# RWKV features and scan in one block: decays inverted tile by tile, scan products waiting for one operand

## Chip, cores and metric

The kernel runs on one core of one Trainium2 chip. The metric is the device time of one execution in microseconds (us). A profile of one execution stands beside it. Engines are named as in the profile: PE (TensorE matmul), PEld (its weight loads), DVE (VectorE), ACT (ScalarE), POOL (GpSimd), SP (SyncE).

## The reference, cut to what matters here

The kernel computes one layer of a hybrid diffusion backbone. The change lies in its RWKV-7 branch, which is run first over 256 context tokens and then over 512 latent tokens, in both time directions. Per token, the features are a decay, a rate `a`, a normalised key `kk` and an effective key:

```
w_log = -softplus(-(w0 + tanh(wd) @ w_up)) - 0.5
decay = exp(-exp(w_log));  a = sigmoid(a0 + ad @ a_up)
kk    = k * k_k, normalised per head of 64
k_eff = k * (1 + (a - 1) * k_a)
step: S = S * decay - (S @ kk) kk*a + v k_eff ;  out = S @ r
```

The context scan yields only a state, which is where the latent scan starts.

## The kernel before, in words

There are 4 `PAIRS` of heads (128 partitions each) and 2 directions, `g` or `z` = 0 and 1. Time is cut into chunks of C = 64 tokens: 4 for the context (names ending in `_c`), 8 for the latent tokens (`_x`).

`phase_rwkv_features` (line 533) works through 8 units n = (z, c), direction 0 first. For each unit PE projects (L596, L598), ACT takes two tanh (L569, L571) and an exponential that is the decay `w` (L577), and DVE runs `decay(n)`, a running product of the decays into `b.G` (L638), and `rates(n)`, which turns `qa` into `(1 + tanh) * kk` (L649). The line for the effective key, `ke`, is made on POOL for direction 0 (L615) and on ACT for direction 1 (L582). Units 4 to 7 are direction 1; DVE does `decay`, `rates` for each in turn. G has 65 columns per chunk, because each product starts with a 1.

`phase_rwkv_scan` (line 675) is a block of its own. Before its first chunk, POOL's `prepare(0, g)` makes for each direction, each product waiting for the one before it: `p` (kk times G, into `pr`), in the latent scan also `rho`, then `kf` (ke times k), and, once DVE has inverted the chunk's G into `ginv` (L991, `reciprocal` over all 4 pairs, 128x256), `q` (qa times ginv, into `qs`) and `k` (kf times ginv, into `ks`), both at L782. Direction 0's products all stand ahead of direction 1's in POOL's queue, and DVE's inversion of direction 1 waits for the `start` that POOL gives behind direction 0's products.

PE then multiplies, in the order Q of g 0, Q of g 1, K of g 0, K of g 1 (L915): Q has `qs` and K has `ks` as stationary operand, both `pr` as moving one. Its waits all stand ahead of the Q product of a direction, and the one on POOL is for that direction's `k`, POOL's last product. Behind them come DVE masks (L1003 to L1012), transposes (L889), five levels of products (L882) and the update of the state (L899, L1036, L1038). Later chunks are prepared while the chunk before is in work, and Q of the next chunk then also waits for the state.

A block ends in a barrier of all engines. The order of work between engines inside a block is set by semaphores: `Steps` counts named results of one engine, so `prep_s[g].wait(pe, i, "k")` waits for POOL's product `k` of chunk i; `scanned`, `normed`, `line_pool` and `line_act` count the units that the features have finished. PSUM tiles and the features' scratch tiles are given up at the end of the features and their places taken by the scan's.

Of the kernel before, what the change touches and what calls it, by code (L numbers as in the profile page):

```python
# [12 lines left out]
F32 = mybir.dt.float32  # L13
# [516 lines left out]
    return np.concatenate([out, out], 0)  # L530


def phase_rwkv_features(nc, a, b, f, T, tag):

    nch = T // C
    with ExitStack() as ctx:
        sb = alloc(nc, ctx)

        def sem(name):
# [6 lines left out]
        first = sb("w65_first" + tag, [P, nch, C + 1])  # L546
        tmp = sb("rw_tmp" + tag, [P, PAIRS, T])
        th = sb("rw_th" + tag, [P, 2, T])
        ps = [ctx.enter_context(nc.psum_tensor(f"ps_rf{k}" + tag, [P, 512], F32)) for k in range(4)]
        ps_n = [ctx.enter_context(nc.psum_tensor(f"ps_rn{k}" + tag, [P, 512], F32)) for k in range(PAIRS)]  # L550
        tanh_wd, half_done, proj = sem("rwf_tanh"), sem("rwf_half"), sem("rwf_proj")
        th_done, dec_done, a_done = sem("rwf_th"), sem("rwf_decay"), sem("rwf_a")
        sq_in, sq_done, norm_mm, norm_max, norm_root = (sem("rwf_kk"), sem("rwf_sq"), sem("rwf_norm"),
                                                        sem("rwf_max"), sem("rwf_sqrt"))
        dve, scanned, slot_done, normed = sem("rwf_dve"), sem("rwf_scanned"), sem("rwf_slot"), sem("rwf_normed")
        line_pool, line_act = sem("rwf_line_pool"), sem("rwf_line_act")
        block = ctx.enter_context(nc.Block())
        units = [(z, c) for z in range(2) for c in range(PAIRS)]

        @block.scalar  # L560
# [57 lines left out]
        @block.vector  # L618
        def _(v):
            link = Count(v, dve)  # L620
            for c in range(PAIRS):
                v.tensor_scalar(b.kk[:, c, 0:T], f[:, 4 + c, :], vecs[:, 4, c:c + 1], None, ALU.mult).then_inc(sq_in, 1)
            v.tensor_scalar(half[:], vecs[:, 0:4, :], 0.5, None, ALU.mult)
            v.tensor_scalar(ka[:, 0], vecs[:, 5, :], 0.5, None, ALU.mult)
            v.tensor_scalar(ka[:, 1], vecs[:, 5, :], -0.5, 1.0, ALU.mult, ALU.add).then_inc(half_done, 1)
            link(v.memset(first[:], 0.0))
            link(v.memset(first[:, :, 0:1], 1.0))
            v.memset(w65[:, :, :, 0:1], 0.0).then_inc(slot_done, 1)

            def decay(n):  # L630
                z, c = units[n]
                v.wait_ge(dec_done, n + 1)
                w = w65[:, c].rearrange("p n t -> p (n t)")
                g = b.G[:, z, c, 0:nch * (C + 1)]
                if z:
                    w, g = w[:, ::-1], g[:, ::-1]

                v.tensor_tensor_scan(out=g, data0=w, data1=first[:].rearrange("p n t -> p (n t)"), initial=0.0,  # L638
                                     op0=ALU.mult, op1=ALU.add).then_inc(scanned, 1)

            def rates(n):
                z, c = units[n]
                v.wait_ge(a_done, n + 1)
                if z == 0:
                    v.wait_ge(line_pool, n + 1)
                else:
                    v.wait_ge(line_act, n - PAIRS + 1)
                qa = b.qa[:, z, c, 0:T]
                v.scalar_tensor_tensor(out=qa, in0=qa, scalar=1.0, in1=b.kk[:, c, 0:T], op0=ALU.add,  # L649
                                       op1=ALU.mult).then_inc(normed, 1)  # L650

            for c in range(PAIRS):
                v.wait_ge(norm_mm, c + 1)
# [12 lines left out]
            v.memset(w65[:, :, :, C:C + 1], 0.0).then_inc(slot_done, 1)  # L666
            v.wait_ge(slot_done, 2)
            for n in range(2, PAIRS):
                rates(n)
            for n in range(PAIRS, 2 * PAIRS):  # L670
                decay(n)
                rates(n)


def phase_rwkv_scan(nc, a, b, f, T, tag, need_out):

# [10 lines left out]
    with ExitStack() as ctx:  # L687
# [5 lines left out]
        def each(name, shape):  # L693
# [1 line left out]

        RW = (3 if need_out else 2) * C
        UN = RW - C
        pr, ginv = each("pr", [P, PAIRS, RW]), each("ginv", [P, PAIRS, C])

        pd, qs, ks, vs, lt, mt = (each(n, [P, PAIRS, C]) for n in ("pd", "qs", "ks", "vs", "lt", "mt"))  # L700
        qt, kt, ti, td, xd = (each(n, [P, PAIRS, C]) for n in ("qt", "kt", "ti", "td", "xd"))
        at, bt, vv, ro = (each(n, [P, PAIRS, C]) for n in ("at", "bt", "vv", "ro"))
        rr, uu, st, tm = (each(n, [P, PAIRS, C]) for n in ("rr", "uu", "st", "tm"))
        lm = each("lm", [P, len(LEVELS), PAIRS, C])
        psw = [[ctx.enter_context(nc.psum_tensor(f"ps_rs{g}{k}" + tag, [P, 2, 512], F32)) for k in range(2)]
               for g in range(2)]

# [14 lines left out]
        gi_s = [Steps(sem(f"rws_gi{g}"), ["gi"]) for g in range(2)]  # L722
# [3 lines left out]
        block = ctx.enter_context(nc.Block())  # L726
# [28 lines left out]
        def _(g_):  # L755
            def prepare(n, g, first=False):
# [10 lines left out]
                if not first:  # L767

                    pe_s[g].wait(g_, n + (-1), "K")
                    copy_s[g].wait(g_, n + (-1), copy_names[-1])  # L770
                g_.sem_inc(turn_g, 1)
                step(g_.tensor_tensor(pr[g][:, :, 0:C], b.kk[:, :, bass.ds(t0, C)], prev, ALU.mult), "p")
                g_.sem_inc(turn_g, 1)
# [98 lines left out]
        def _(pe):  # L872
# [32 lines left out]
            def body(i, more):  # L905
                for k, buf in enumerate((qs, ks)):
                    for g in range(2):
                        if k == 0:
                            prep_s[g].wait(pe, i, prep_names[-1])

                            dve_s[g].wait_last(pe, i)
                            act_s[g].wait_last(pe, i)
                        pe.sem_inc(turn, 1)
# [62 lines left out]
        def _(v):  # L976
# [11 lines left out]
            def inverse(n, g):  # L988

                prep_s[g].wait_last(v, n)  # L990
                gi_s[g].mark(v.reciprocal(ginv[g][:], b.G[:, g, :, bass.ds(start_of(n, g, C + 1, 1 - g), C)]))  # L991

            for g in range(2):
                gi_s[g].start(v)
                inverse(0, g)

            def body(i, more):
                for g in range(2):
# [1766 lines left out]
def build_program(nc, a, out):  # L2765
    with ExitStack() as ctx:
# [24 lines left out]
        with mixers:  # L2791
# [33 lines left out]
            with ExitStack() as rw:  # L2825
# [3 lines left out]
                b.qa = gone("qa", [P, 2, PAIRS, TX])  # L2829
                b.G = gone("G", [P, 2, PAIRS, TX // C * (C + 1)])  # L2830
                b.state = gone("rw_state", [P, 2, PAIRS, C])
                phase_rwkv_features(nc, a, b, b.fC, TC, "_c")
                phase_rwkv_scan(nc, a, b, b.fC, TC, "_c", False)
                phase_rwkv_features(nc, a, b, b.fX, TX, "_x")
                b.rwo = sr("rwo", [P, 2, PAIRS, TX])
                phase_rwkv_scan(nc, a, b, b.fX, TX, "_x", True)
                spent.close()
                b.clear_semaphores(nc)
                late = alloc(nc, ctx, "right")
# [116 lines left out]
```

## Time and profile before

| what | value |
|---|---|
| median of 3 runs | 2667.61 us (2666.59 to 2672.57) |
| the profiled execution | 2667.66 us |
| its span in the trace | 2665.9 us |
| PE busy, share of span | 2519.4 us, 95% |
| DVE busy, share of span | 1309.2 us, 49% |
| ACT / POOL busy | 1020.5 us / 850.1 us |
| context features, first to last instruction | 334.03 to 353.31 us |
| latent features | 468.72 to 498.43 us |

The times of the trace count from the start of its span. In a timeline row the columns are start, duration, engine, line, operation, output and inputs, shapes, count, and in brackets how long the engine stood idle before it and which work ended that. A row with a count above 1 is a merged stretch, so its duration is that of all of them together.

### The profile page before, as it was taken

The page shows a single profiled execution, that of the slowest core. Times are in us where ns is not written, and L with a number is a line of the kernel's source. Part 1 is how long each engine was busy: PE and PEld are TensorE (multiplying, and loading weights), DVE is VectorE, ACT ScalarE, POOL GpSimd, SP SyncE. Part 2 cuts the span into 40 slices and gives each one's busy share as a digit, 9 for nine tenths or more (in the row PEclk, how much of TensorE's full clock was granted, in tenths as well). Part 3 has the DMA queues.
Part 4 walks back from the last instruction along what each step waited for, and adds up shares of the span by engine and source line. Part 5 has one row for each costly group of instructions (what it writes and reads, how often), then busy time and mean ns, then how long its engine had stood idle before and what let it go on. Part 6 is the DMA issues. An engine that isn't in the chain of part 4 may idle for free.

```text
span 2665.9 us, 53106 instructions
## 1 busy us (share of the span) xinstructions
PE 2519.4 (95%) x19732; PEld 2078.4 (78%) x19732; DVE 1309.2 (49%) x2662; ACT 1020.5 (38%) x1725; POOL 850.1 (32%) x689
## 2 busy tenths in 40 slices
PE   7999669699999989999999999989999999999997
PEld 3885469499967867887888888878888888888886
DVE  5765655656553327997444444400044444444443
ACT  4222453533352233223666666632322322232222
POOL 2420243444554445645555555524400000000001
PEclk8999889799999999999999999999999999999999
DMA  6541000000032324234355444464455555555551
GB/s 263 188 174 40 1 2 1 2 0 0 1 145 89 94 71 143 85 100 144 115 205 181 169 169 169 169 236 142 134 196 197 190 189 189 191 196 196 194 197 64
DMA packets 163913, 348.64 MB, mean 131 GB/s; under 512 B 13368, under 2 KB 79416, under 8 KB 161664
## 3 DMA queue, kind: packets, MB, share of 16 engines
q1 hardware_dynamic: 163840, 347.65, 37.7%
q8 instruction: 48, 0.79, 0.1%
q14 instruction: 25, 0.20, 0.0%
HBM read 276.30 MB, written 71.30 MB: 130 GB/s over the span
## 4 chain that ended last, share of the span: by engine, by line
PE 53%; DVE 5%; issue 1%; DMA 1%; POOL 1%; ACT 1%; SPq 0%; DVEq 0%; ACTq 0%; POOLq 0%
PE ps_a L85 9%; PE ps_a L86 9%; PE ps_a L87 9%; PE ps_y L85 7%; PE ps_y L86 7%; PE ps_y L87 7%; PE ps_w L2535 4%; DVE cand L2328 0%; DVE top_ix L2311 0%; DMA w_scratch<-w_block 0%; DVE top_ix L2324 0%; DVE scores_left L2314 0%; DVE picked L2385 0%; DVE pick L2369 0%; DVE pick L2152 0%
## 5 line engine op out<-in xcount | busy, mean ns | idle before, releaser
L2711 DVE TENSOR_TENSOR v_lo<-v_raw,v_hi 128x1024 fp32r<-128x1024 f32 x128 | 158.3, 1237 | 542.2 <-ACT v_hi L2663 542.2
L85 PE MATMUL ps_a<-h_hi,u_hi 128*128 128x512 f32 x1024 | 412.0, 402 | 8.2 <-ACT act L2056 7.7
L86 PE MATMUL ps_a<-h_hi,u_lo 128*128 128x512 f32 x1024 | 405.7, 396 | 0.0
L87 PE MATMUL ps_a<-h_lo,u_hi 128*128 128x512 f32 x1024 | 405.7, 396 | 0.0
L2663 ACT ACTIVATE v_hi<-v_raw 128x1024 fp32r<-128x1024 f32 x128 | 135.8, 1061 | 478.4 <-PE ps_a L87 470.0
L85 PE MATMUL ps_y<-gated_hi,v_hi 128*128 128x512 f32 x768 | 299.5, 390 | 3.1 <-DVE gated_lo L2713 3.1
L87 PE MATMUL ps_y<-gated_lo,v_hi 128*128 128x512 f32 x768 | 299.3, 390 | 0.0
L86 PE MATMUL ps_y<-gated_hi,v_lo 128*128 128x512 f32 x768 | 299.2, 390 | 0.0
L2056 ACT ACTIVATE act<-ps_a 128x512 f32<-128x512 f32 x128 | 76.5, 597 | 414.0 <-PE ps_a L87 397.4
L85 PEld LDWEIGHTS ps_a<-h_hi,u_hi 128*128 128x128 f32 x1024 | 194.0, 189 | 52.4 <-issue 8.5
L2699 POOL TENSOR_TENSOR v_raw<-v_raw 128x512 f32<-128x512 f32 x6 | 7.7, 1288 | 711.7 <-ACT v_raw L2683 711.7
L87 PEld LDWEIGHTS ps_a<-h_lo,u_hi 128*128 128x128 f32 x1024 | 193.4, 189 | 46.0
L86 PEld LDWEIGHTS ps_a<-h_hi,u_lo 128*128 128x128 f32 x1024 | 193.9, 189 | 43.1
L2516 POOL TENSOR_SCALAR mixed<-iota,w_token 128x128 f32<-128x128 f32 x128 | 151.4, 1183 | 218.2 <-PE ps_w L2535 202.4
L2040 POOL TENSOR_TENSOR u_lo<-u_raw,u_hi 128x1024 fp32r<-128x1024 f32 x64 | 156.3, 2445 | 181.6 <-ACT u_hi L2036 181.6
L2040 DVE TENSOR_TENSOR u_lo<-u_raw,u_hi 128x1024 fp32r<-128x1024 f32 x64 | 78.5, 1226 | 251.4 <-ACT u_hi L2036 251.4
L85 PEld LDWEIGHTS ps_y<-gated_hi,v_hi 128*128 128x128 f32 x768 | 144.5, 188 | 33.5 <-DVE v_lo L2711 3.5
L87 PEld LDWEIGHTS ps_y<-gated_lo,v_hi 128*128 128x128 f32 x768 | 144.5, 188 | 30.1
L86 PEld LDWEIGHTS ps_y<-gated_hi,v_lo 128*128 128x128 f32 x768 | 144.5, 188 | 30.0
L2036 ACT ACTIVATE u_hi<-u_raw 128x1024 fp32r<-128x1024 f32 x128 | 134.4, 1050 | 40.8 <-DMA u_raw<-in_uT 40.8
L2567 ACT ACTIVATE w_block<-ps_w 128x512 f32 x128 | 141.2, 1103 | 0.0
L1077 POOL TENSOR_TENSOR mg_w_lo<-mg_raw,mg_w_hi 128x1024 fp32r<-128x1024 f32 x38 | 94.0, 2475 | 126.9 <-ACT mg_w_hi L1073 126.9
(524 smaller groups left out, 5417.4 us busy)
## 6 DMA issues: line engine op xcount, KB each, us to landing
u_raw<-in_uT SPq DMA_DIRECT2D x128, 512.0 KB, 3.6
v_raw<-in_v SPq DMA_DIRECT2D x128, 512.0 KB, 4.8
a_scratch<-act SPq DMA_DIRECT2D x128, 256.0 KB, 2.1
w_scratch<-w_block SPq DMA_DIRECT2D x8, 4096.0 KB, 12.2
w_ring<-w_scratch SPq DMA_DIRECT2D x64, 512.0 KB, 4.4
gated<-a_scratch SPq DMA_DIRECT2D x128, 256.0 KB, 4.8
mg_raw<-in_w_merge SPq DMA_DIRECT2D x36, 512.0 KB, 3.6
vM<-in_ada_rows SPq DMA_DIRECT2D x32, 512.0 KB, 4.9
```

The costliest lines, as they stand in the source:

```text
L85: pe.matmul(out, wh, xh, start=first, stop=False)
L86: pe.matmul(out, wl, xh, start=False, stop=False)
L87: return pe.matmul(out, wh, xl, start=False, stop=last)
L1077: g.tensor_tensor(self.wl[:, k], self.raw[:, k], self.wh[:, k], ALU.subtract).then_inc(self.w_lo, 1)
L2036: act.activation(self.uh[:, q], self.raw[:, q % 2], ACT.Copy).then_inc(self.hi, 1)
L2040: eng.tensor_tensor(self.ul[:, q], self.raw[:, q % 2], self.uh[:, q], ALU.subtract).then_inc(self.lo, 1)
L2056: act.activation(self.act[:, q % 2], self.ps[q % 2][:], ACT.Gelu).then_inc(self.out, 1)
L2516: g_.tensor_scalar(oi[:, s, SUB - 1], iota, cur[:, s, 0:1], cur[:, s, 1:2], ALU.is_equal, ALU.mult).then_inc(built_p, 1)
L2535: m = pe.matmul(ps[s][:, k, :], oi[:, s, k], oj[:, s, k], start=True, stop=True)
L2567: act.activation(wb[:, half, :, bass.ds(g * BODY + dt, SUB)].rearrange("p j t -> p t j"), ps[s][:], ACT.Copy).then_inc(evac[s], 1)
L2663: act.activation(vh[:, q], v_raw[:, q], ACT.Copy).then_inc(v_hi, 1)
L2711: v.tensor_tensor(vl[:, q], v_raw[:, q], vh[:, q], ALU.subtract).then_inc(v_lo, 1)
```

## The change

Features and scan of one token stream share one block, so the barrier between them is gone, for the context and for the latent stream. An object `ScanEntry` holds what both sides need. `ginv` is allocated outside and is written in the features' loop: in units 4 to 7 DVE inverts, besides `decay(n)` and `rates(n)`, the first chunk's 64 columns of one pair of direction 0 and one pair of direction 1, so there are 8 inversions of 128x64 in place of 2 of 128x256. POOL's first products now wait for `scanned`, `normed` and the `ke` line of their direction, 4 units for direction 0 and 8 for direction 1. PE waits for `q` ahead of each Q product and for `k` ahead of each K product, in every chunk. The order of allocation is changed, so that the scan's tiles which are written early don't lie over scratch that the features still use.

```diff
+class ScanEntry:
+    def __init__(self, nc, b, tag, ginv):
+        def sem(name):
+            return b.semaphore(nc, name + tag)
+        self.ginv = ginv
+        self.gi_s = [Steps(sem(f"rws_gi{g}"), ["gi"]) for g in range(2)]
+        self.scanned, self.normed = sem("rwf_scanned"), sem("rwf_normed")
+        self.line_pool, self.line_act = sem("rwf_line_pool"), sem("rwf_line_act")

-def phase_rwkv_features(nc, a, b, f, T, tag):
+def phase_rwkv_features(nc, a, b, f, T, tag, block, entry):
...
+        ps_n = [... psum_tensor(f"ps_rn{k}" + tag ...) for k in range(PAIRS)]
         ps = [... psum_tensor(f"ps_rf{k}" + tag ...) for k in range(4)]
-        ps_n = [... psum_tensor(f"ps_rn{k}" + tag ...) for k in range(PAIRS)]
...
-        block = ctx.enter_context(nc.Block())
...
             v.wait_ge(slot_done, 2)
             for n in range(2, PAIRS):
                 rates(n)
+            def inverse(g, c):
+                v.wait_ge(scanned, g * PAIRS + c + 1)
+                o = (1 - g) if g == 0 else (nch - 1) * (C + 1)
+                return v.reciprocal(entry.ginv[g][:, c], b.G[:, g, c, o:o + C])
+            for g in range(2):
+                entry.gi_s[g].start(v)
             for n in range(PAIRS, 2 * PAIRS):
                 decay(n)
+                m = inverse(0, n - PAIRS)
+                if n == 2 * PAIRS - 1:
+                    entry.gi_s[0].mark(m)
                 rates(n)
+                m = inverse(1, n - PAIRS)
+                if n == 2 * PAIRS - 1:
+                    entry.gi_s[1].mark(m)

-def phase_rwkv_scan(nc, a, b, f, T, tag, need_out):
+def phase_rwkv_scan(nc, a, b, f, T, tag, need_out, block, entry):
...
-        pr, ginv = each("pr", [P, PAIRS, RW]), each("ginv", [P, PAIRS, C])
...
+        pr, ginv = each("pr", [P, PAIRS, RW]), entry.ginv
...
+                if first:
+                    g_.wait_ge(entry.scanned, (g + 1) * PAIRS)
+                    g_.wait_ge(entry.normed, (g + 1) * PAIRS)
+                    g_.wait_ge(entry.line_act if g else entry.line_pool, PAIRS)
                 g_.sem_inc(turn_g, 1)
                 step(g_.tensor_tensor(pr[g][:, :, 0:C], b.kk[:, :, bass.ds(t0, C)], prev, ALU.mult), "p")
...
                 for k, buf in enumerate((qs, ks)):
                     for g in range(2):
+                        prep_s[g].wait(pe, i, "k" if k else "q")
                         if k == 0:
-                            prep_s[g].wait(pe, i, prep_names[-1])
                             dve_s[g].wait_last(pe, i)
                             act_s[g].wait_last(pe, i)
...
-            for g in range(2):
-                gi_s[g].start(v)
-                inverse(0, g)
...
-                phase_rwkv_features(nc, a, b, b.fC, TC, "_c")
-                phase_rwkv_scan(nc, a, b, b.fC, TC, "_c", False)
+                ginv = [sr(f"ginv{g}", [P, PAIRS, C]) for g in range(2)]
+                with nc.Block() as block:
+                    entry = ScanEntry(nc, b, "_c", ginv)
+                    phase_rwkv_features(nc, a, b, b.fC, TC, "_c", block, entry)
+                    phase_rwkv_scan(nc, a, b, b.fC, TC, "_c", False, block, entry)
```

The latent stream's two calls are put into one block in the same way.

## Rows read from the trace of the kernel before

**Rows 1.** Stretches, all engines; columns: from:to, length, busy times, clock, DMA
```profile
362.10:366.30 4.20, 4.16 (x48) 4.19 (x50) 1.27 (x3) 0.80 (x3) 1.89 (x3) 0.61 0.02 4
...
508.70:514.30 5.60, 5.55 (x48) 4.83 (x50) 1.94 (x5) 1.23 (x5) 1.63 (x3) 0.69 0.02 4
```

**Rows 2.** Waits by cause, each scan; columns: us in total, times, longest
```profile
PE ps_rs_c L915 <- POOL ks_c L782: 10.3, 2, 8.5
...
PE ps_rs_x L915 <- POOL ks_x L782: 13.3, 2, 11.5
```

**Rows 3.** Timeline, PE, first chunk of each scan
```profile
362.14 1.97 PE L915 MATMUL ps_rs_c<-pr_c,qs_c 64*64 64x128 f32 x16 [1.77 <-POOL ks_c L782]
...
508.75 2.82 PE L915 MATMUL ps_rs_x<-pr_x,qs_x 64*64 64x192 f32 x16 [1.84 <-POOL ks_x L782]
511.34 3.18 PE L915 MATMUL ps_rs_x<-pr_x,ks_x 64*64 64x192 f32 x32
514.34 0.64 PE L889 MATMUL ps_rs_x<-unit,td_x 64*64 64x64 f32 x16
514.80 0.64 PE L889 MATMUL ps_rs_x<-unit,vs_x 64*64 64x64 f32 x16
515.27 0.64 PE L889 MATMUL ps_rs_x<-unit,td_x 64*64 64x64 f32 x16
```

**Rows 4.** Timeline, DVE, end of the context features and start of the scan
```profile
347.53 0.69 DVE L638 TENSOR_TENSOR_SCAN G<-w_c,w_first_c 128x260 f32<-128x260 f32 x1
348.14 0.40 DVE L649 SCALAR_TENSOR_TENSOR qa<-qa,kk 128x256 f32<-128x256 f32 x1
349.07 0.70 DVE L638 TENSOR_TENSOR_SCAN G<-w_c,w_first_c 128x260 f32<-128x260 f32 x1 [0.53 <-ACT w_c L577]
...
354.50 1.75 DVE L991 RECIPROCAL ginv_c<-G 128x256 f32<-128x256 f32 x1
```

**Rows 5.** Timeline, POOL, the context scan's first products
```profile
356.43 0.72 POOL L782 TENSOR_TENSOR qs_c<-qa,ginv_c 128x256 f32<-128x256 f32 x1 [0.94 <-DVE ginv_c L991]
357.33 0.72 POOL L782 TENSOR_TENSOR ks_c<-ks_c,ginv_c 128x256 f32<-128x256 f32 x1 [0.18 <-POOL qs_c L782]
358.47 0.73 POOL L772 TENSOR_TENSOR pr_c<-kk,G 128x256 f32<-128x256 f32 x1 [0.41 <-POOL ks_c L782]
...
361.27 0.73 POOL L782 TENSOR_TENSOR ks_c<-ks_c,ginv_c 128x256 f32<-128x256 f32 x1 [0.18 <-POOL qs_c L782]
```

**Rows 6.** Timeline, DVE, end of the latent features and start of the scan
```profile
489.61 1.23 DVE L638 TENSOR_TENSOR_SCAN G<-w_x,w_first_x 128x520 f32<-128x520 f32 x1
490.76 0.67 DVE L649 SCALAR_TENSOR_TENSOR qa<-qa,kk 128x512 f32<-128x512 f32 x1
...
494.14 1.24 DVE L638 TENSOR_TENSOR_SCAN G<-w_x,w_first_x 128x520 f32<-128x520 f32 x1 [0.64 <-ACT w_x L577]
...
500.19 1.75 DVE L991 RECIPROCAL ginv_x<-G 128x256 f32<-128x256 f32 x1
```

**Rows 7.** Timeline, POOL, the latent scan's first products
```profile
502.13 0.72 POOL L782 TENSOR_TENSOR qs_x<-qa,ginv_x 128x256 f32<-128x256 f32 x1 [0.68 <-DVE ginv_x L991]
...
507.88 0.73 POOL L782 TENSOR_TENSOR ks_x<-ks_x,ginv_x 128x256 f32<-128x256 f32 x1 [0.18 <-POOL qs_x L782]
```

**Rows 8.** Groups by line and shape, DVE's reciprocals; busy, mean ns
```profile
L991 DVE RECIPROCAL ginv_x<-G 128x256 f32 x14 | 23.5, 1719 | 0.0
...
L1748 DVE RECIPROCAL ml_dn<-ml_dn 128x4 f32<-128x4 f32 x8 | 1.4, 178 | 0.3
L2399 DVE RECIPROCAL soft_total<-soft_total 128x32 f32<-128x32 f32 x1 | 0.4, 353 | 0.0
```

**Rows 9.** Timeline, DVE, rates while POOL makes its lines
```profile
344.46 1.00 DVE L649 SCALAR_TENSOR_TENSOR qa<-qa,kk 128x256 f32<-128x256 f32 x2
...
483.78 1.75 DVE L649 SCALAR_TENSOR_TENSOR qa<-qa,kk 128x512 f32<-128x512 f32 x2
```

**Rows 10.** One line's instructions, L615 on POOL; ns min/median/max
```profile
L615 POOL TENSOR_SCALAR ke<-qa,rw_ka_c x4: 559/710/1745, 336.9 to 345.1; 128x256 f32<-128x256 f32 x4
```

More of the change, by code:

```diff
@@ L548, in phase_rwkv_features @@
         th = sb("rw_th" + tag, [P, 2, T])
+        ps_n = [ctx.enter_context(nc.psum_tensor(f"ps_rn{k}" + tag, [P, 512], F32)) for k in range(PAIRS)]
         ps = [ctx.enter_context(nc.psum_tensor(f"ps_rf{k}" + tag, [P, 512], F32)) for k in range(4)]
-        ps_n = [ctx.enter_context(nc.psum_tensor(f"ps_rn{k}" + tag, [P, 512], F32)) for k in range(PAIRS)]
         tanh_wd, half_done, proj = sem("rwf_tanh"), sem("rwf_half"), sem("rwf_proj")
@@ L554, in phase_rwkv_features @@
                                                         sem("rwf_max"), sem("rwf_sqrt"))
-        dve, scanned, slot_done, normed = sem("rwf_dve"), sem("rwf_scanned"), sem("rwf_slot"), sem("rwf_normed")
-        line_pool, line_act = sem("rwf_line_pool"), sem("rwf_line_act")
-        block = ctx.enter_context(nc.Block())
+        dve, slot_done = sem("rwf_dve"), sem("rwf_slot")
+        scanned, normed, line_pool, line_act = entry.scanned, entry.normed, entry.line_pool, entry.line_act
         units = [(z, c) for z in range(2) for c in range(PAIRS)]
@@ L697, in phase_rwkv_scan @@
         UN = RW - C
-        pr, ginv = each("pr", [P, PAIRS, RW]), each("ginv", [P, PAIRS, C])
[L700 to L703, printed above, removed]
+        lt, mt, qt, kt, ti, td, xd = (each(n, [P, PAIRS, C]) for n in ("lt", "mt", "qt", "kt", "ti", "td", "xd"))
+        at, bt, vv, rr, uu, tm = (each(n, [P, PAIRS, C]) for n in ("at", "bt", "vv", "rr", "uu", "tm"))
         lm = each("lm", [P, len(LEVELS), PAIRS, C])
+        pd, qs, ks, vs, ro, st = (each(n, [P, PAIRS, C]) for n in ("pd", "qs", "ks", "vs", "ro", "st"))
+        pr, ginv = each("pr", [P, PAIRS, RW]), entry.ginv
         psw = [[ctx.enter_context(nc.psum_tensor(f"ps_rs{g}{k}" + tag, [P, 2, 512], F32)) for k in range(2)]
@@ L721, in phase_rwkv_scan @@
         level_s = [Steps(sem(f"rws_level{g}"), [f"m{s}" for s in LEVELS]) for g in range(2)]
-        gi_s = [Steps(sem(f"rws_gi{g}"), ["gi"]) for g in range(2)]
+        gi_s = entry.gi_s
         copy_s = [Steps(sem(f"rws_copy{g}"), copy_names) for g in range(2)]
@@ L725, in phase_rwkv_scan @@
         turn, turn_g, bonus_in = sem("rws_turn"), sem("rws_turn_pool"), sem("rws_bonus")
-        block = ctx.enter_context(nc.Block())
         def start_of(i, g, stride, base=0):
@@ L2831, in build_program @@
                 b.state = gone("rw_state", [P, 2, PAIRS, C])
-                phase_rwkv_features(nc, a, b, b.fC, TC, "_c")
-                phase_rwkv_scan(nc, a, b, b.fC, TC, "_c", False)
-                phase_rwkv_features(nc, a, b, b.fX, TX, "_x")
-                b.rwo = sr("rwo", [P, 2, PAIRS, TX])
-                phase_rwkv_scan(nc, a, b, b.fX, TX, "_x", True)
+                ginv = [sr(f"ginv{g}", [P, PAIRS, C]) for g in range(2)]
[3 more added lines that the diff above has]
+                    phase_rwkv_scan(nc, a, b, b.fC, TC, "_c", False, block, entry)
+                with nc.Block() as block:
+                    entry = ScanEntry(nc, b, "_x", ginv)
+                    phase_rwkv_features(nc, a, b, b.fX, TX, "_x", block, entry)
+                    b.rwo = sr("rwo", [P, 2, PAIRS, TX])
+                    phase_rwkv_scan(nc, a, b, b.fX, TX, "_x", True, block, entry)
                 spent.close()
```

## The prediction

> **What bounds the kernel now.** I read the page first (PE is busy nearly all the span, so the change can only give what PE waits for), then the waits by cause for each scan, then the timeline of each engine from the features' end to PE's third group of products, and last the groups by shape for the price of a reciprocal. In the waits the reader is to see that PE stood still for POOL's product `ks` exactly twice in each scan [rows 2]: both times in the first chunk, once ahead of Q of direction 0 and once ahead of Q of direction 1. From then on PE and the engines that feed it follow each other, and no later chunk waits for POOL's `k`. So what counts is when Q of direction 1 starts in the first chunk: at 362.14 in the context scan and at 508.75 in the latent one [rows 3]. Q of direction 0 ran earlier, and PE idled 1.77 and 1.84 us behind it; moving that product alone gives nothing.
>
> What releases Q of direction 1 is one chain: DVE's 256-wide inversion of direction 0 ends at 356.25 [rows 4], POOL starts `q` 0.18 later, then `k`, then all of direction 1's products one by one, the last ending at 362.00 [rows 5]. In the latent scan the inversion ends at 501.94 [rows 6], `q` starts at 502.13 and the last `k` ends at 508.61 [rows 7]. DVE's second inversion lies beside POOL and is not waited for. Hence two levers: the time at which direction 0's `ginv` is ready, and which of POOL's last two products PE waits for.
>
> **The change part by part.**
>
> *One operand.* PE's wait ahead of Q of direction 1 moves from `k` to `q`. One POOL product takes 0.72 and the next starts 0.90 behind it [rows 5], so Q starts 0.90 earlier in each scan: 1.80 together. The K products now wait for `k`. K of direction 1 stands behind 16 instructions of Q and those of K of direction 0, several us against the 0.90 that `k` needs, so the `k` is there. These waits are also added in the other chunks, two for each; transposes of direction 0 start at 514.34 and 514.80 with no wait between, those of direction 1 at 515.27 behind three satisfied waits and a semaphore update: 0.47 against 0.46 [rows 3]. I take them as nothing.
>
> *Inversions in the loop.* The trace has no 64-wide reciprocal. 4, 32 and 256 columns take 178, 353 and 1719 to 1753 ns [rows 4, 8]: 6.2 ns a column both between the first two and between the last two, so 64 columns come to 0.55. Bounds from rows: above 0.353, below 1.75. I take 0.55 because the three shapes lie on one line. An instruction starts 0.08 before the one ahead of it ends (scan at 347.53 of 0.69, rates at 348.14 [rows 4]), so an inversion adds 0.47.
>
> Context: a unit is then 0.61 + 0.47 + 0.32 (rates of 0.40) + 0.47 = 1.87. Before, units came every 1.5 to 1.6 and DVE waited 0.53 for ACT in each [rows 4], so this idle time is used up and DVE becomes the engine that sets the loop. Unit 4 starts at 347.53 as before; three units, a scan and an inversion later direction 0's `ginv` is done: 347.53 + 5.61 + 0.61 + 0.55 = 354.30. Against 356.25 that is 1.95 earlier; the removed barrier, the two memsets and the wide inversion are all in this difference.
>
> Latent: 1.15 + 0.47 + 0.59 + 0.47 = 2.68 against a loop in which DVE idled 0.64 a unit for ACT [rows 6]. 489.61 + 8.04 + 1.15 + 0.55 = 499.35 against 501.94: 2.59 earlier.
>
> *POOL's first products, moved into DVE's loop.* With the barrier gone, `p` and `kf` (in the latent scan `rho` too) of direction 0 run beside units 4 and 5 instead of ahead of `q`. For `q` this is free: in the context scan they ended before the inversion anyway. But they meet DVE's scans and rates. The line instruction of POOL took 0.56 when alone and up to 1.75 beside DVE [rows 10], and DVE paid too: two rates took 1.00 where 0.32 + 0.40 = 0.72 was due, 0.28 more; in the latent features 1.75 where 0.59 + 0.67 = 1.26 was due, 0.49 more [rows 4, 6, 9]. DVE's inversions have only one input, and the wide ones ran beside POOL's products at 1.75 and 0.72 [rows 4, 5]. I take 0.28 a product, as the products are 256 wide: 2 x 0.28 = 0.56 and 3 x 0.28 = 0.84. Bounds: nothing, if each finds an inversion to run beside; and 0.73 each, a whole product of [rows 5], 1.46 and 2.19.
>
> The Trainium skill says more of this (SBUF — State Buffer, Who interferes with whom): a VectorE instruction with two SBUF inputs and a GpSimd instruction that reads SBUF exclude each other for the whole instruction. The lengthened rows agree in kind; by the page as it stands each early product would cost DVE up to its full length, which is the third case below.
>
> *`q` meets the last rates.* Behind the inversion of direction 0 in unit 7 DVE goes on with rates (7), 0.40 or 0.67 long and started 0.08 before the inversion ends. POOL's `q` would start 0.18 after it ends, so it can be held by 0.32 - 0.18 = 0.14 and 0.59 - 0.18 = 0.41. Bounds: nothing and these. I take these.
>
> *What is queued behind.* PE's Q also waits for DVE's `start` of the scan, now behind the last inversion of direction 1: 0.32 + 0.47 after direction 0's, while `q` is ready 0.18 + 0.72 after it, so it hides. POOL's `p` of direction 1 waits for rates (7), done 0.3 to 0.6 after `ginv` and 1.98 before `p` is due. ACT's copies come earlier. The state copy in the latent scan lies in the 4.7 us between Q of direction 0 and direction 1. No DMA is in flight worth naming in these stretches (4 GB/s, [rows 1]), so what PE gains it keeps to the end.
>
> *Sum.* Context 1.95 - 0.56 - 0.14 + 0.90 = 2.15. Latent 2.59 - 0.84 - 0.41 + 0.90 = 2.24. Together 4.4. The profiled execution took 2667.66 against a median of 2667.61, so 2663.3 for either.
>
> On the overlap of 0.08 the Trainium skill reads otherwise at first (VectorE: DVE Perf Modes, The DRAIN you can't avoid): the next VectorE op waits until the pipe is empty, unless it is one that isn't held. The row at 348.14 shows the earlier start. Without it the 13 joints ahead of the last inversion of direction 0 would cost 1.04 in each stream and the gain would be 2.3.
>
> *The clock.* PE ran these first products at 1.2 GHz: its granted clock was 0.61 and 0.69 in the stretches that begin with Q of direction 1, full only at their end [rows 1]. At the low level 16 instructions took 2.82, then 32 took 3.18 [rows 3], so a microsecond there does some 0.56 of the work. I assume that the rise comes earlier with the products. If it stayed where it is, 2.2 us more in each scan would run low, costing about 1.0 each.
>
> **The rivals.**
>
> 1. *Forecast: about half of each advance survives*, 2663.3. Chance 0.45, of which 0.03 above 5.3 us gain.
> 2. *Nothing meets anything*: the products run beside the inversions, `q` isn't held. 4.4 + 1.4 + 0.55 = 6.35, 2661.3; with a cheaper reciprocal (0.353) ACT sets the loop again and some 2.3 more come, 2659.0. For it: inversions fill half the joints of DVE's loop. Against it: both rows of lengthened rates. Chance 0.31.
> 3. *POOL's early products hold DVE in full*, 0.73 each: 4.4 - 2.25 = 2.1, 2665.5; with the clock's rise left behind, 2667.5. For it: the 0.49 of a single meeting; against it the 0.28 of a meeting of this width. Joints without overlap in DVE's loop (0.08 each, 2.1 in all) would give 2665.4, and are counted here: the start at 348.14 [rows 4] speaks against them. The two rules of the Trainium skill named above are those by which it would come out so. Chance 0.18.
> 4. *The other side: the narrow reciprocal is dear.* 7 inversions stand ahead of direction 0's last result in each stream, 14 in all, on an engine that now sets the loop. At 0.87 each (half a wide one) the gain is gone, from 0.55 + 9.7 / 14 = 1.24 the kernel is slower by over 5.3 us, and at 1.75 it would be 14 x 1.20 - 4.4 = 12.4 slower, 2680. Against it stand the three shapes on one line. Chance 0.06.
>
> **Numbers.** 0.2% is 5.3 us, about what a measurement of this kernel can tell from no change. The likeliest case lies just inside it. Faster: rival 2 and the 0.03, 0.34. Slower: 0.06. Within: 0.60. The range leaves out the far ends of rivals 2 and 3 and all of 4: 2659.5 to 2667.3. The likeliest case's own is 2662.2 to 2665.
>
> **What would show it.** Of the step of the one operand: Q of direction 1 starts 0.1 to 0.2 behind the end of its `q`, not `k`. Of the inversions: 8 a stream at 0.55, no idle time of DVE for ACT in units 5 to 7 of the context, direction 0's last done 1.3 to 1.4 (context) and 1.7 to 1.8 (latent) before the times above. Of the meeting: scans or rates longer than 0.70/0.40 and 1.24/0.67 while `p`, `rho`, `kf` run. Of the sum: Q of direction 1 at 2.15 and 2.24 before 362.14 and 508.75. The prediction is wrong if a reciprocal is well off 0.55, if PE has another wait between Q and the transposes, or if the clock's rise moves by more than the products do.

## The result and the profile after

| | before | after |
|---|---|---|
| median | 2670.09 us (2666.59 to 2672.59, 4 runs) | 2733.72 us (2732.31 to 2735.74, 4 runs) |
| profiled execution | 2667.66 us | 2733.04 us |
| its span | 2665.9 us | 2731.2 us |

The changed kernel is slower: the ratio is 1.024, with a 95% interval of 1.0222 to 1.0258. I had forecast 2663.3, within 2659.5 to 2667.3.

The step that was argued at length came out, and better than forecast. Timeline of PE in the changed kernel, start of both scans, the rows that answer to [rows 3]:

```profile
360.43 1.97 PE L941 MATMUL ps_rs_c<-pr_c,qs_c 64*64 64x128 f32 x16 [1.88 <-POOL qs_c L809]
...
503.50 2.82 PE L941 MATMUL ps_rs_x<-pr_x,qs_x 64*64 64x192 f32 x16 [1.97 <-POOL qs_x L809]
506.08 3.48 PE L941 MATMUL ps_rs_x<-pr_x,ks_x 64*64 64x192 f32 x32
509.38 0.64 PE L916 MATMUL ps_rs_x<-unit,td_x 64*64 64x64 f32 x16
```

PE now waits for `qs`, and in the latent scan Q of direction 1 starts at 503.50 in place of 508.75. The loss lies behind it. ACT's last copy of the scan's output starts at 812.19 in the changed kernel and at 746.56 in the one before, so from that Q on the latent scan takes 308.7 us in place of 237.8: 70.9 more, less the 5.2 won ahead of it, is the 65.6 by which the rest of the kernel comes later (the spans differ by 65.3).

What PE waits for there, in the waits by cause of the changed kernel from 503.5 to 812.6 (columns: us in total, times, longest):

```profile
PE ps_rs_x L941 <- issue: 37.9, 6, 6.8
PE ps_rs_x L926 <- issue: 9.1, 14, 1.2
PE ps_rs_x L909 <- issue: 4.4, 9, 0.9
PE ps_rs_x L941 <- POOL qs_x L809: 2.0, 1, 2.0
```

and in the kernel before from 508.7 to 746.8:

```profile
PE ps_rs_x L882 <- issue: 2.4, 6, 0.8
PE ps_rs_x L915 <- POOL ks_x L782: 1.8, 1, 1.8
PE ps_rs_x L899 <- issue: 1.0, 2, 0.8
```

Six times, ahead of the first product of a repeat of PE's loop over the chunks, PE stood 6.3 us on average for no engine ("issue"). Nothing of the kind is in the kernel before. One repeat from its start to the next, timeline of PE in the changed kernel:

```profile
542.72 5.38 PE L941 MATMUL ps_rs_x<-pr_x,qs_x 64*64 64x192 f32 x32 [6.75 <-issue]
...
583.64 5.38 PE L941 MATMUL ps_rs_x<-pr_x,qs_x 64*64 64x192 f32 x32 [6.30 <-issue]
588.79 3.09 PE L941 MATMUL ps_rs_x<-pr_x,ks_x 64*64 64x192 f32 x32
591.70 0.51 PE L916 MATMUL ps_rs_x<-unit,td_x 64*64 64x64 f32 x11
```

A repeat is 583.64 - 542.72 = 40.92 us long. The same 32 products take 5.38 behind the stall where 2.8 is normal (below). The granted clock was 1.00 in the 5.3 us ahead of the idle time and 0.92 over it (572.00 to 577.30 and 577.30 to 583.60), and it is low behind it. Stretches of the changed kernel (from:to, length, busy us of PE, PEld, DVE, ACT, POOL, granted clock, DMA share, GB/s):

```profile
583.20:592.00 8.80, 8.36 (x75) 7.19 (x77) 3.20 (x9) 1.70 (x5) 1.89 (x3) 0.65 0.01 2
592.00:617.40 25.40, 23.10 (x732) 22.12 (x730) 12.33 (x24) 7.85 (x22) 12.19 (x18) 1.00 0.02 4
```

The last piece is in the DMA queues, a part of the page that I had not read for the forecast. Queue `q8 instruction` of the changed kernel:

```profile
q8 instruction: 102, 1.67, 0.2%
```

and of the one before:

```profile
q8 instruction: 48, 0.79, 0.1%
```

1.67 MB in 102 packets is 16.4 KB each, which I take as 16,384 bytes. 54 more packets of instructions were fetched, which is 9 for each of the six jumps back to the loop's start. The same queue's row for the latent scan alone, changed kernel from 503.5 to 812.6:

```profile
q8 instruction: 67, 1.10, 1.5%
```

and the kernel before from 508.7 to 747:

```profile
q8 instruction: 14, 0.23, 0.4%
```

67 - 14 = 53 of the 54 lie here. In PE's built program the part from behind the register set that opens the latent scan's loop to its closing branch is 1,729 instructions long in both kernels. It begins at instruction 4858 before and at 4853 after: merging the blocks drops 6 barrier and branch instructions of PE ahead of it, and the changed waits add 1 (12,464 against 12,459 in all; these counts are from the built programs, and no trace shows them). A packet of 16,384 bytes is 256 instructions at the program's 64 bytes each, so 1,729 instructions are 6.75 packets, and where such a stretch begins decides whether it touches 7 or 8 of them. All of PE's program before is 48.7 packets, and the queue's row has 48, so I read this queue as PE's.

The theory that I tested: **the place in PE's program**. 5 instructions fewer ahead of the loop put it across an eighth packet, its instructions no longer stay in place, and each repeat fetches them anew. Rivals: the new **waits** (two for each direction and chunk in place of one) upset PE's issue; or something of the **merged block** itself (inversions, tiles' places, semaphores) does, wherever the loop lies.

### The profile page after: what moved, and what is told of

It reads as the page before. It is cut to its first block, busy times and chain, and to the rows that moved or that the text cites. A ratio compares the mean times of both kernels' runs of the same rounds, so it can differ in the third digit from the quotient of the medians.

```text
span 2731.2 us, 53103 instructions
## 1 busy us (share of the span) xinstructions
PE 2542.0 (93%) x19732; PEld 2090.6 (77%) x19732; DVE 1310.0 (48%) x2674; ACT 1019.8 (37%) x1725; POOL 847.3 (31%) x689
## 3 DMA queue, kind: packets, MB, share of 16 engines
q8 instruction: 102, 1.67, 0.2%
## 4 chain that ended last, share of the span: by engine, by line
PE 51%; DVE 5%; issue 1%; DMA 1%; POOL 1%; ACT 1%; SPq 0%; DVEq 0%; ACTq 0%; POOLq 0%
PE ps_a L85 9%; PE ps_a L86 9%; PE ps_a L87 9%; PE ps_y L85 6%; PE ps_y L86 6%; PE ps_y L87 6%; PE ps_w L2557 4%; DVE cand L2350 0%; DVE top_ix L2333 0%; DMA w_scratch<-w_block 0%; DVE top_ix L2346 0%; DVE scores_left L2336 0%; DVE picked L2407 0%; DVE pick L2391 0%; DVE pick L2174 0%
## 5 line engine op out<-in xcount | busy, mean ns | idle before, releaser
L2557 PEld LDWEIGHTS ps_w<-mixed 128*128 128x128 f32 x1024 | 125.8, 194 | 10.3 <-POOL mixed L2538 5.0
```

The lines of the kernel that those rows point to most:

```text
L2557: m = pe.matmul(ps[s][:, k, :], oi[:, s, k], oj[:, s, k], start=True, stop=True)
```

## The experiments

"Begins" says how many instructions PE's latent loop lies behind its place in the kernel before. All times of a group are from one chip; the kernel before was run on it too, and its median stands with the group.

### First group: place, or waits (before: 2669.99 us, 2662.80 to 2676.38)

**after_pad8**: the changed kernel with 8 semaphore updates on PE, which nothing waits for, ahead of the latent features' projections. Begins +3.

```diff
+            if T == TX:
+                for _ in range(8):
+                    pe.sem_inc(pad, 1)
             pe.wait_ge(tanh_wd, 1)
```

> The changed kernel with 8 more semaphore updates in PE's latent features, ahead of the loop over chunks; no result depends on them. Placement theory (the lost time is PE's instructions being fetched anew in every chunk of the latent loop, because that loop now begins 5 instructions earlier in PE's program): the loop begins 3 instructions later than in the kernel before, the instruction queue falls from 102 packets to about 48, PE's 6 to 7 us of issue idle per chunk go, and the time is 2661 to 2665 us. Added-wait theory (the two more waits of PE in every chunk cost the time): nothing changes, 2734 us. Dear-inversion theory (the inversions in the features' loop): nothing changes, 2734 us.

Measured: 2660.96 us (2656.50 to 2666.07, 12 runs), ratio 0.9975 (0.9965 to 0.9986); profiled 2658.77. The whole loss is gone, and what is left is faster than before. Its instruction queue on the page and its waits of PE from 500.4 to 737.2:

```profile
q8 instruction: 48, 0.79, 0.1%
```

```profile
PE ps_rs_x L913 <- issue: 2.4, 6, 0.8
PE ps_rs_x L945 <- POOL qs_x L813: 2.0, 1, 2.0
PE ps_rs_x L930 <- issue: 0.2, 1, 0.2
```

One repeat in the timeline of its PE, without a stall, and the clock in its first products:

```profile
560.87 2.82 PE L945 MATMUL ps_rs_x<-pr_x,qs_x 64*64 64x192 f32 x32
563.49 2.80 PE L945 MATMUL ps_rs_x<-pr_x,ks_x 64*64 64x192 f32 x32
566.09 0.66 PE L920 MATMUL ps_rs_x<-unit,td_x 64*64 64x64 f32 x16
...
590.04 2.17 PE L945 MATMUL ps_rs_x<-pr_x,qs_x 64*64 64x192 f32 x24
```

```profile
560.87:566.09 5.22, 5.22 (x65) 5.22 (x67) 4.37 (x10) 1.97 (x7) 0.79 (x2) 1.00 0.00 0
```

A repeat takes 590.04 - 560.87 = 29.17, so a refetch costs 40.92 - 29.17 = 11.75 us: 6.30 of idle time ahead of Q; 2.84 because Q and K run at the lower clock (8.06 from Q to the transposes against 5.22); and inside the repeat (9.1 + 4.4 - 2.4 - 0.2) / 6 = 1.8 of short waits for issue. 0.8 stays over. Six repeats are 70.5 us. By the same two marks the latent scan takes 236.6 us in after_pad8 (500.46 to 737.04), so the changed kernel's is 72.1 longer than this one, and 70.9 longer than the one before.

The Trainium skill (Runtime: NRT & Kernel Launch, Instruction fetch mechanics) says that an engine's instruction memory is refilled in blocks of 16 KiB, 256 instructions, that PE's holds 2048 of them, and that a taken branch to something outside the window forces a fetch before execution goes on. The packets of 16,384 bytes and the stall behind each jump back agree with it. It also calls the window two pages; here a loop of 6.75 blocks was kept in this kernel, so for PE the measurement decides against that.

**after_kwait**: the changed kernel with PE's waits as before, all ahead of Q, for `k`. Begins -6.

```diff
-                        prep_s[g].wait(pe, i, "k" if k else "q")
                         if k == 0:
+                            prep_s[g].wait(pe, i, prep_names[-1])
```

> The changed kernel with PE's waits put back as they were (k alone, ahead of each Q product), the rest of the change kept. Placement theory: the latent loop begins 6 instructions earlier than in the kernel before, so about 102 instruction packets and 2733 to 2737 us. Added-wait theory: back to about 2665 us. Dear-inversion theory: 2734 us.

Measured: one run, 2731.77 us, 102 packets, and the same stall without the new waits:

```profile
PE ps_rs_x L941 <- issue: 36.6, 6, 6.5
```

The rival of the waits falls: without the new waits the stall stays, and after_pad8 has them and no stall.

**before_split**: the kernel before with only the changed waits. Begins +1.

```diff
+                        prep_s[g].wait(pe, i, "k" if k else "q")
                         if k == 0:
-                            prep_s[g].wait(pe, i, prep_names[-1])
```

> The kernel before with only PE's waits changed: q ahead of each Q product, k ahead of each K product. Placement theory: the latent loop begins 1 instruction later than in the kernel before, so nothing is fetched anew; 1.8 us faster (0.90 in each scan), 2665.8. Added-wait theory: 60 us or more slower.

Measured: 2664.75 us (12 runs), ratio 0.9983 (0.9970 to 0.9996), 48 packets. From the start of unit 4's running product to Q of direction 1 it takes 13.91 in the context and 18.25 in the latent scan, against 14.61 and 19.14 before: 0.70 and 0.89 for the one-operand wait.

**before_pad64**: the kernel before with 64 such updates at the same place as in after_pad8. Begins +64.

```diff
+                for _ in range(64):
+                    pe.sem_inc(pad, 1)
```

> The kernel before with 64 more semaphore updates on PE ahead of the latent loop, in the latent features. Placement theory: the loop begins 64 instructions later; 1,729 long, it then lies over one more block of 256 instructions than before if it now begins right behind a block's start, so the instruction queue rises to about 100 packets and the time to 2725 to 2745 us, with nothing else of the change in it. Both other theories: no change, at most 3 us for the updates, 2667 to 2671 us.

Measured: one run, 2676.49 us, 48 packets. My expectation of a refetch was wrong. If the block's edge lies where after_pad4 puts it (below), this loop's last 2 to 5 instructions lie in an eighth block, and it is kept all the same. The time above the median is the updates themselves: unit 4's running product starts at 498.01 in place of 489.61 [rows 6].

### Second group: the slow place without the change (before: 2667.93 us, 2663.22 to 2673.14)

**before_pad251**: the kernel before with 251 updates between the latent features' last product and the scan. Begins +251, which is -5 and a whole block.

```diff
             for n in range(2, len(units)):
                 project(n)
+            if T == TX:
+                for _ in range(251):
+                    pe.sem_inc(pad, 1)
```

> The kernel before with 251 more semaphore updates on PE between the latent features' last product and the latent scan. 251 instructions later is, in blocks of 256, the same place as 5 earlier, where the changed kernel's loop begins. Placement theory: about 100 instruction packets, PE's issue idle of 6 to 7 us ahead of Q in chunks 2 to 7 of the latent scan, some 70 us more than the updates themselves cost (64 of them cost about 9 us, so these up to 35, of which some 11 lie in PE's idle time): 2755 to 2770 us. Theories in which an added wait or an inversion costs the time: only the updates, 2690 us.

Measured: one run, 2767.19 us. The kernel before, with its barrier, two wide inversions and old waits, now has the changed kernel's stall in size and number:

```profile
PE ps_rs_x L919 <- POOL ks_x L786: 44.8, 2, 43.0
PE ps_rs_x L919 <- issue: 37.2, 6, 6.5
```

103 packets, one of which is the longer program's own, and repeats of 39.8 us on average (Q at 583.26 and, five repeats on, at 782.46). From Q of direction 1 to the last output copy it is 301.1 us (545.24 to 846.34), 63.3 more than before. The other 36 us of the loss are the updates themselves, which hold PE ahead of the scan. The rival of the merged block falls with it.

**before_pad128**: the same with 128. Begins +128, which is far from the block edge at which the loop began.

```diff
-                for _ in range(251):
+                for _ in range(128):
```

> The kernel before with 128 more semaphore updates on PE, in the same place. If the loop of 1,729 instructions must lie in 7 blocks of 256: it now lies in 8, so about 100 packets and 70 us more than the updates, 2745 us. If what counts is only whether the loop's first instruction falls just ahead of a block's start: 48 packets, and only the updates, some 2670 to 2680 us.

Measured: one run, 2720.87 us, 102 packets, and from Q of direction 1 (519.35) to the scan's last output copy 277.6 us against 237.8 before. That is 6.6 a repeat and not 11.75, and the time is well under the 2745 that I expected. Its stall is shorter:

```profile
PE ps_rs_x L919 <- issue: 27.1, 6, 4.9
```

So the loop is refetched at a second place too, where it reaches 66 to 69 instructions into an eighth block (189 to 192 in the changed kernel). A refetch was cheaper here: 4.5 us ahead of Q, 6.3 in the changed kernel.

**after_pad4**: the changed kernel with 4 updates instead of 8. Begins -1.

```diff
-                for _ in range(8):
+                for _ in range(4):
```

> The changed kernel with 4 more semaphore updates on PE ahead of the latent loop, which then begins 1 instruction earlier than in the kernel before. If the block's start falls exactly on the place where the loop of the kernel before begins: 102 packets, 2733 us. If it lies 2 to 5 instructions ahead of it: 48 packets, 2661 us.

Measured: one run, 2665.21 us, 48 packets. The edge lies within the 4 instructions between this place and that of the changed kernel.

**pad8_wide**: after_pad8 with one wide inversion for each direction behind the last unit. Begins +3.

```diff
-            def inverse(g, c):
-                v.wait_ge(scanned, g * PAIRS + c + 1)
+            def inverse(g):
+                v.wait_ge(scanned, (g + 1) * PAIRS)
...
+            for g in range(2):
+                entry.gi_s[g].mark(inverse(g))
```

> The changed kernel with the 8 updates that put the latent loop back in place, and with direction 0's and direction 1's first inversion made 256 wide behind the features' last unit instead of tile by tile in their loop; one block, early POOL products and split waits stay. By my terms of the prediction: context, direction 0's ginv is done at unit 4's start plus 5.8 (as before) plus 1.7 = 7.5 us, against 6.6 in after_pad8 and 8.7 before; latent, 10.5 against 9.5 and 12.3. So Q of direction 1 comes 0.9 and 1.0 us later than in after_pad8: 2662.9 against 2661. If the narrow inversions were the whole gain: 2668.

Measured: 2665.92 us (12 runs), ratio 0.9991 (0.9982 to 1.0000). Unit 4 to Q of direction 1: 12.53 and 16.49. Against after_pad8's 11.67 and 15.77 the narrow inversions are worth 0.86 and 0.72 at this mark. Against before_split's 13.91 and 18.25 the merged block alone, with no barrier and POOL's first products made early, is worth 1.38 and 1.76. The time is above the 2662.9 that I expected, but against the kernel before on each one's chip the intervals of the two ratios still touch, so the whole times don't settle what the inversions give.

### Third group: the loop's length, and the small terms (before: 2669.71 us, 2664.65 to 2672.04)

**after_short**: the changed kernel, its loop at the changed kernel's place, with fewer products in each repeat: in the latent scan PE leaves out two of the three terms of the output's product and one of the two of the state's, so it computes something else. The loop is 1,537 instructions long.

```diff
-                        pe_s[g].mark(each_sum(g, 0, 0, (st[g], ro[g]), (vv[g], at[g]), (uu[g], bt[g])))
+                        pe_s[g].mark(each_sum(g, 0, 0, (st[g], ro[g])))
-                    pe_s[g].mark(each_sum(g, 1, 1, (kt[g], vv[g]), (qt[g], uu[g])))
+                    pe_s[g].mark(each_sum(g, 1, 1, (kt[g], vv[g]), *([] if need_out else [(qt[g], uu[g])])))
```

> The changed kernel with the latent scan leaving out two of the three terms of its output product and one of the two of its state product on PE (48 of 416 products a chunk), so its output differs. PE's loop begins where it does in the changed kernel, but has 1,537 instructions in place of 1,729. If the loop's reach over blocks of 256 instructions counts, it now ends in the 7th block: 48 packets, no issue idle ahead of Q, a chunk of some 26.5 us (29.2 less 48 products at 0.06), and 2731 - 66 - 7 x 2.8 = 2640 us or a little more. If a beginning just ahead of a block's start is itself the trouble: 102 packets less those of the shorter body, chunks of 38 us, 2710 us.

Measured: one run, 2646.61 us, 46 packets, repeats of 26.7 us with no stall for issue:

```profile
590.31 2.82 PE L941 MATMUL ps_rs_x<-pr_x,qs_x 64*64 64x192 f32 x32 [0.36 <-DVE st_x L1060]
...
617.03 2.82 PE L941 MATMUL ps_rs_x<-pr_x,qs_x 64*64 64x192 f32 x32 [0.36 <-DVE st_x L1060]
```

The same beginning with a shorter reach is kept, so it is how far the loop reaches over the blocks that counts, and not where its first instruction lies.

**pad8_order**: after_pad8 with POOL's first `k` of both directions behind the `q` of both.

```diff
+                if not first:
+                    last_product(n, g)
...
+            for g in range(2):
+                last_product(0, g)
```

> The changed kernel with the 8 updates, and POOL's product k of both directions in the first chunk moved behind q of both. By the chain of the prediction Q of direction 1 starts 0.9 us earlier in each scan than in after_pad8, and k is ready 0.9 and 1.8 us behind q while Q of direction 1 takes 2.0 or 2.8 us: 1.8 us faster than after_pad8, 0.9968 of the kernel before. If POOL's levels, which come 0 to 1.8 us later, are what PE waits for: no gain over after_pad8, 0.9975.

Measured: 2661.86 us (9 runs), ratio 0.9978 (0.9968 to 0.9989). Q of direction 1 comes 0.90 and 0.94 earlier, at 10.77 and 14.83 behind unit 4, but the time is that of after_pad8 within the noise. Timeline of PE in the latent scan:

```profile
500.40 2.83 PE L953 MATMUL ps_rs_x<-pr_x,qs_x 64*64 64x192 f32 x16 [1.04 <-POOL qs_x L812]
502.99 4.02 PE L953 MATMUL ps_rs_x<-pr_x,ks_x 64*64 64x192 f32 x32
506.82 0.64 PE L928 MATMUL ps_rs_x<-unit,td_x 64*64 64x64 f32 x16
```

From Q to the transposes it is 6.42 us here and 6.04 in after_pad8 (500.46 to 506.50): the K products are longer, 4.02 against 3.64, so 0.38 of the 0.94 is given back. By Q of the next chunk, 46.87 behind unit 4 here and 47.00 there, 0.13 is left. That it is the clock's rise, left behind by the products, is argued from these lengths and was not tried by itself.

**pad8_hold**: after_pad8 with POOL's first products of direction 0 waiting for all 8 units.

```diff
-                    g_.wait_ge(entry.scanned, (g + 1) * PAIRS)
-                    g_.wait_ge(entry.normed, (g + 1) * PAIRS)
+                    g_.wait_ge(entry.scanned, 2 * PAIRS)
+                    g_.wait_ge(entry.normed, 2 * PAIRS)
```

> The changed kernel with the 8 updates, and POOL's first products of direction 0 held until all 8 units are done, so that they can't meet DVE's loop. By the prediction's term for the meeting (0.56 and 0.84) direction 0's ginv comes that much earlier after unit 4's start than in after_pad8 (6.57 and 9.50 us there); by the clean units seen there (1.73 and 2.54) only 0.3 and 0.3. Against it the products then stand ahead of q, 1.8 and 2.7 us: Q of direction 1 starts 1.3 to 2.4 us later.

Measured: one run, 2675.88 us. Its unit 4 in the context already starts 8.3 us later than in after_pad8 (355.20 against 346.86), so only its distances are read. Direction 0's `ginv` is done 6.33 and 9.29 us behind unit 4's start; with POOL's early products beside it, in after_pad8, 6.57 and 9.50. The meeting costs 0.24 and 0.21. From unit 4 to Q of direction 1 it is 13.60 and 18.58: making the products early is worth 1.9 and 2.8 (I had expected 1.3 to 2.4), far more than the meeting takes.

**pad8_kwait**: after_kwait with 9 updates. Begins +3.

```diff
+                for _ in range(9):
+                    pe.sem_inc(pad, 1)
```

> The changed kernel with PE's waits put back to k alone, and 9 updates so that the latent loop begins 3 instructions later than in the kernel before. Q of direction 1 starts 0.90 us later after unit 4's start than in after_pad8 (11.67 and 15.77 us there), 48 packets. If the split waits cost anything in the later chunks, these are shorter than 29.2 us.

Measured: one run, 2663.73 us, 48 packets, unit 4 to Q of direction 1 12.58 and 16.66, that is 0.91 and 0.89 more than after_pad8. With after_kwait this is the 2 x 2 table of wait and place: only the place moves the time by 68 us.

## Why the prediction was wrong

**The step that failed** is the price of the removed barrier, of which the forecast says that it is "all in this difference", the time at which `ginv` is ready, and with it the end of the path, "what PE gains it keeps to the end". I priced the instructions that the edits put in and take out by the time in which they execute. The edits also move all of PE's later code, by -5 instructions at the latent loop: -6 from the barrier and +1 from the changed waits (after_kwait begins at -6, before_split at +1). That loop was 6.75 blocks long and, if the edge is at its start, began within 4 instructions of it. The scan gave back 70.9 us. Of the added waits the forecast says "I take them as nothing", and this holds: a repeat takes 29.2 us with them in after_pad8 and without them in pad8_kwait. No rival contained it. The range's bounds were all built from engines waiting for engines; the mechanism lies in none of them, and costs 12 us in each of six repeats. What the forecast gave as its own signs of failure ("another wait between Q and the transposes") looked in the first chunk, and the first chunk has no jump back.

The hint was on the page of the kernel before: 48 packets of instructions, of which 14 in the latent scan. 14 packets are 3,584 instructions, and the loop's seven passes alone are 12,103. So the loop was kept, and there was something to lose.

**The steps by themselves**, as distances from the start of unit 4's running product in DVE's queue to Q of direction 1:

| | before | forecast | after | after_pad8 |
|---|---|---|---|---|
| context | 14.61 | 12.46 | 11.68 | 11.67 |
| latent | 19.14 | 16.90 | 15.76 | 15.77 |

The advance is 2.93 + 3.38 = 6.3 us, and not 4.4. That it comes so near rival 2's 6.35 is luck: a meeting of 0.45 and a hold of 0.2 are in it, which that rival has at nothing, and a loop 0.9 cheaper than forecast. Timeline of DVE in the changed kernel, the answers to [rows 4, 6]:

```profile
348.75 0.69 DVE L650 TENSOR_TENSOR_SCAN G<-w_c,w_first_c 128x260 f32<-128x260 f32 x1
349.36 0.53 DVE L686 RECIPROCAL ginv<-G 128x64 f32<-128x64 f32 x1
...
354.26 0.63 DVE L650 TENSOR_TENSOR_SCAN G<-w_c,w_first_c 128x260 f32<-128x260 f32 x1
354.81 0.52 DVE L686 RECIPROCAL ginv<-G 128x64 f32<-128x64 f32 x1
355.25 0.35 DVE L661 SCALAR_TENSOR_TENSOR qa<-qa,kk 128x256 f32<-128x256 f32 x1
...
487.74 1.23 DVE L650 TENSOR_TENSOR_SCAN G<-w_x,w_first_x 128x520 f32<-128x520 f32 x1
...
495.63 1.17 DVE L650 TENSOR_TENSOR_SCAN G<-w_x,w_first_x 128x520 f32<-128x520 f32 x1
496.73 0.52 DVE L686 RECIPROCAL ginv<-G 128x64 f32<-128x64 f32 x1
497.17 0.62 DVE L661 SCALAR_TENSOR_TENSOR qa<-qa,kk 128x512 f32<-128x512 f32 x1
```

- *The reciprocal.* 0.52 to 0.54 where 0.55 was read off the line through three shapes. Right; rival 4 falls.
- *The loop.* Without POOL beside it, 6.33 and 9.29 against the forecast's 6.77 and 9.74: 0.45 too dear in each. A clean unit takes 1.73 and 2.54, not 1.87 and 2.68: behind an inversion a running product takes 0.63 and 1.17 and a `rates` 0.35 and 0.62, while the rows I took, 0.69 and 0.40, 1.23 and 0.67, stand behind a `rates` and a running product. POOL isn't the cause, as it was silent beside those rows too, and in pad8_hold, with POOL silent, unit 4's running product behind a `rates` still takes 0.69 and 1.23. Why the predecessor matters is not shown. DVE never waits for ACT in units 5 to 7, as forecast.
- *The meeting.* 0.24 and 0.21, forecast 0.56 and 0.84. The rows of [rows 9] met a longer line of another form. Rival 3 with its full hold falls, by a factor of 6 and 10 in price. But the meeting wasn't cheap for POOL: its early `p`, `rho` and `kf` of the latent scan took 1.50, 0.87 and 1.44 (rows below) where before they took 0.73, 0.67 and 0.73, 1.7 us more in all. POOL bore the most of it, and nothing waited for POOL there.
- *`q` held.* Timeline of POOL in the changed kernel, the answers to [rows 5, 7]:

```profile
355.51 0.72 POOL L809 TENSOR_TENSOR qs_c<-qa,ginv 128x256 f32<-128x256 f32 x1 [4.64 <-DVE ginv L686]
...
359.56 0.72 POOL L809 TENSOR_TENSOR qs_c<-qa,ginv 128x256 f32<-128x256 f32 x1 [0.27 <-POOL ks_c L804]
...
487.99 1.50 POOL L799 TENSOR_TENSOR pr_x<-kk,G 128x256 f32<-128x256 f32 x1 [2.77 <-DVE qa L661]
489.67 0.87 POOL L802 TENSOR_TENSOR pr_x<-fX,G 128x256 f32<-128x256 f32 x1 [0.18 <-POOL pr_x L799]
490.71 1.44 POOL L804 TENSOR_TENSOR ks_x<-ke,fX 128x256 f32<-128x256 f32 x1 [0.18 <-POOL pr_x L802]
...
497.42 0.94 POOL L809 TENSOR_TENSOR qs_x<-qa,ginv 128x256 f32<-128x256 f32 x1 [5.27 <-DVE ginv L686]
498.55 0.75 POOL L809 TENSOR_TENSOR ks_x<-ks_x,ginv 128x256 f32<-128x256 f32 x1 [0.18 <-POOL qs_x L809]
...
502.63 0.73 POOL L809 TENSOR_TENSOR qs_x<-qa,ginv 128x256 f32<-128x256 f32 x1 [0.28 <-POOL ks_x L804]
```

  In the context nothing is held (355.33 to 355.51); in the latent scan `q` starts on time but takes 0.94, and `k` follows 1.13 behind it and not 0.90. It costs 0.2, forecast 0.41.
- *The one operand.* PE's Q of direction 1 starts 0.15 and 0.14 behind the end of its `q`. Worth 0.91 and 0.89 by pad8_kwait, forecast 0.90. Right.
- *The clock.* "I assume that the rise comes earlier with the products" is too good for the first products: from Q to the transposes the latent scan takes 5.59 before, 5.88 in the changed kernel and 6.04 in after_pad8. The price of a rise left behind was taken from 32 products in 3.18 as full speed; 2.8 is full speed (after_pad8), so a microsecond at the low level does some half of the work and not 0.56.
- *What the gain is worth.* after_pad8 differs from the changed kernel by 8 instructions that nothing waits for, so it is what the change does at a harmless place: 0.25% (0.14 to 0.35%) or 6.7 us (3.7 to 9.3), which holds both the 4.4 of the forecast and the 6.3 of the distances. How much of a distance at Q reaches the end is not shown part by part. Q of the next chunk comes 43.87 and 51.61 behind unit 4 before, and 39.64 and 47.00 in after_pad8. But before_pad64, with the code of before from unit 4 on, has 42.88 and 50.27, so one execution can't tell parts of 0.7 to 0.9 us apart there.

**What stays open.** Where exactly the limit lies: 64 more are kept and 128 more are not. The kept places go from -1 to +64, which is two more than a loop of 1,729 can have within seven blocks, and which end of the loop has that slack is not shown. Why the idle time of a refetch differs from 4.5 to 6.3 us with the place. And the 0.8 us of a repeat above.

**The version to keep** is after_pad8: ratio 0.9975 (0.9965 to 0.9986) to the kernel before. pad8_order is no better.

## What to carry to other kernels

When an edit adds or drops any instruction of PE ahead of a long loop, count the loop's instructions and look where it begins and ends before and after. The one of 1,729 instructions here touches seven or eight blocks of 256 by its place, and the one of 1,537 was kept; longer loops and other engines were not tried. A few instructions that nothing waits for can move a loop back. In the profile read the instruction queue's packets: more of them than before, with waits for "issue" at the loop's first instruction, meant here that the loop was fetched anew in each repeat, and the cost was the stall, the lower clock behind it and short gaps within. To price an edit apart from its place, compare it with the edit plus padding, and read distances between marks inside one run rather than whole times.

## What the runs showed of the hardware

- A PE loop of 1,729 instructions was kept over its repeats at the places -1 to +3, where it touches 7 blocks of 256 instructions, and at +64. In four kernels in which it reached well into an eighth, 54 or 55 packets more were fetched, 9 a repeat, and PE stood 4.5 to 6.3 us on average in each. A loop of 1,537 instructions that begins at the changed kernel's place was kept.
- Behind the idle time ahead of a repeat the granted clock was lower: 1.00 ahead of it, 0.65 over the next 8.8 us, a mean of its levels of 1.2 and 2.4 GHz, then 1.00; 32 products took 5.38 in place of 2.82.
- Updates of a semaphore are not free on PE: 64 of them moved unit 4 of the latent features by 8.4 us (489.61 to 498.01).
- POOL's 256-wide products beside DVE's running products, rates and inversions cost DVE 0.24 us for two of them and 0.21 for three. The three took POOL 3.81 us together, against 2.13 in the kernel before.
